# Stick-breaking scores in plain fp32 on the two row halves of TensorE, their first blocks ahead of the former sums, and a reordered last norm

## The reference

```python
def stick_breaking_mixer(h, w_qkv, w_o):
    ...
        z = einsum('bqhd,bshd->bhqs', q_blk, k) * scale
        valid = key_pos[None, :] < q_pos[:, None]
        log_beta = log_sigmoid(z)
        log_keep = where(valid, log_sigmoid(-z), 0.0)
        log_keep_after = cumsum(log_keep, axis=3, reverse=True) - log_keep
        att = where(valid, exp(log_beta + log_keep_after), 0.0)
        return einsum('bhqs,bshd->bqhd', att, v)
    ...

def _rmsnorm(x, g):
    y = x * rsqrt(mean(x * x, axis=-1, keepdims=True) + 1e-6)
    return y * g
```

## Time and profile before

| | |
|---|---|
| time, median of 3 runs | 1160.87 us (1160.63 to 1161.13) |
| profiled execution | 1160.88 us |
| its span | 1159.0 us |
| instructions | 17713 |
| PEld, DVE, ACT, POOL busy | 88%, 70%, 55%, 24% of the span |
| weights and inputs read | 198.43 MB, 172 GB/s over the span |

### The profile page before, as it was taken

One profiled execution on the slowest core, in us unless ns is written; L12 is line 12 of the kernel. 1 busy time (PEld: TensorE's weight loads), 2 busy tenths in 40 slices (PEclk: granted clock), 3 DMA queues, 4 the chain that ended last, 5 costly groups with the idle time before them and its releaser, 6 DMA issues.

```text
span 1159.0 us, 17713 instructions
## 1 busy us (share of the span) xinstructions
PE 1147.4 (99%) x7180; PEld 1020.5 (88%) x7180; DVE 806.4 (70%) x881; ACT 633.2 (55%) x753; POOL 273.2 (24%) x257
## 2 busy tenths in 40 slices
PE   8999999999999999999999999999999999999997
PEld 7999888888998888888899888888889998888885
DVE  6776877776588677767658767777546868777742
ACT  6776565564455456555346656555436765655632
POOL 2000533231123444221111353221110005332100
PEclk9999999999999999999999999999999999999999
DMA  9432655565563255555554355555554326555550
GB/s 341 175 110 74 221 193 199 187 202 190 191 204 110 104 187 182 184 188 198 193 182 146 110 184 191 201 187 182 185 185 176 110 73 220 188 199 193 197 185 37
DMA packets 31515, 201.75 MB, mean 174 GB/s; under 512 B 3680, under 2 KB 5280, under 8 KB 8016
## 3 DMA queue, kind: packets, MB, share of 16 engines
q1 hardware_dynamic: 29088, 196.88, 47.5%
q10 hardware_dynamic: 2032, 3.07, 1.0%
q0 software_dynamic: 320, 0.72, 0.3%
HBM read 198.43 MB, written 1.25 MB: 172 GB/s over the span
## 4 chain that ended last, share of the span: by engine, by line
PE 96%; DVE 2%; DMA 1%; SPq 1%; ACT 0%; issue 0%; POOL 0%; ACTq 0%; DVEq 0%
PE banks L1345 41%; PE banks L1349 21%; PE banks L1333 8%; PE banks L1339 6%; PE banks L1340 6%; PE banks L1341 6%; PE banks L1501 1%; PE banks L1417 1%; PE banks L1515 1%; DMA raw<-w 1%; PE banks L1657 1%; PE banks L1684 1%; PE banks L1669 1%; PE banks L1503 0%; PE banks L1655 0%; SPq L327 0%
## 5 line engine op out<-in xcount | busy, mean ns | idle before, releaser
L869 DVE TENSOR_TENSOR w_lo<-raw,w_hi 128x2048 fp32r<-128x2048 f32 x180 | 442.2, 2461 | 187.9 <-ACT w_hi L509 187.6
L509 ACT ACTIVATE w_hi<-raw 128x2048 fp32r<-128x2048 f32 x183 | 348.5, 1907 | 62.1 <-PE banks L1333 23.4
L1345 PE MATMUL banks<-x_split,w_hi 128*128 128x512 f32 x1408 | 336.8, 391 | 0.0
L1345 PEld LDWEIGHTS banks<-x_split,w_hi 128*128 128x128 f32 x1408 | 258.5, 188 | 50.2 <-DVE w_lo L869 0.4
L1349 PEld LDWEIGHTS banks<-x_split,w_lo 128*128 128x128 f32 x1408 | 181.0, 191 | 7.1
L1349 PE MATMUL banks<-x_split,w_lo 128*128 128x256 f32 x1408 | 184.0, 283 | 0.0
L1345 PE MATMUL banks<-hid_split,w_hi 128*128 128x512 f32 x528 | 129.9, 392 | 0.0
L1345 PEld LDWEIGHTS banks<-hid_split,w_hi 128*128 128x128 f32 x528 | 95.6, 188 | 17.5
L1339 PE MATMUL banks<-x_split,w_hi 128*128 128x256 f32 x384 | 110.0, 286 | 0.0
L1340 PE MATMUL banks<-x_split,w_hi 128*128 128x256 f32 x384 | 108.6, 283 | 0.0
L1341 PE MATMUL banks<-x_split,w_lo 128*128 128x256 f32 x384 | 108.6, 283 | 0.0
(11 more groups left out here) (204 smaller groups left out, 1627.4 us busy)
## 6 DMA issues: line engine op xcount, KB each, us to landing
raw<-w SPq DMA_DIRECT2D x183, 1024.0 KB, 4.9
raw<-w SPq DMA_DIRECT2D x8, 256.0 KB, 5.4
raw<-w SPq DMA_DIRECT2D x2, 512.0 KB, 7.4
k_all<-k_all ACTq DMA_DIRECT2D x1, 960.0 KB, 8.0
x<-x_in SPq DMA_DIRECT2D x4, 128.0 KB, 5.2
x<-x_in SPq DMA_DIRECT2D x2, 256.0 KB, 7.0
rel_bias<-rel_scratch POOLq DMA_DIRECT2D x8, 64.0 KB, 3.1
y_gain<-final_rows ACTq DMA_DIRECT2D x1, 512.0 KB, 6.4
```

What stands on the lines that cost most here:

```text
L509: act.activation(w_hi[u % HI_SLOTS][:, :], raw[slot][:, :], ACT.Copy).then_inc(hi_done, 1)
L869: dve.tensor_tensor(w_lo[slot][:, :], raw[slot][:, :], w_hi[u % HI_SLOTS][:, :].bitcast(FP32), ALU.subtract).then_inc(lo_done, 1)
L1345: return pe.matmul(pair(b), wt[0], xs, start=first, stop=False, skip_group_check=True)
```

## The change

Scores: the splits of keys and queries, their tiles, signals and the zero fill go. Each of the six blocks of 128 x 128 is a plain fp32 matmul of a head's own 64 partitions, `k_all` by `q_all`. The columns are laid out anew, 384 in each of two banks: bank 0 holds the three blocks early keys x early queries of head 0, the same of head 1, and late keys x late queries of head 0; bank 1 holds early keys x late queries of head 0, the same of head 1, and late keys x late queries of head 1. The masks, the sums, ACT's and DVE's operations and the values follow this layout. Two of the six blocks (`logits_begun(p + 1)`, with the masks) now stand ahead of `keep_sums(p)`, and the other four (`logits_rest(p + 1)`) behind it. Last norm: ACT squares all four halves and makes both guesses ahead of any scaling, the mean is one operation with the first half's part done ahead, DVE scales three of the four halves and ACT the fourth, and SyncE stores three.

```diff
...
@@ -239,8 +237,12 @@
-        def head_blocks(v):
-            return v.rearrange("p (h b q) -> p h b q", h=2, b=2)
+        def stick_scores(p):
+            return two_banks[p % 2][:, :].rearrange("p (b s) -> p b s", b=2)[:, :, 0:384]
+        def stick_rows(v):
+            return v.rearrange("p (b s) -> p b s", b=2)
...
@@ -343,9 +345,10 @@
-            for t in range(2):
-                sp.wait_ge(out_ready, t + 1)
-                sp.dma_start(out[:, t, 0:512], y_rows[:, t, 0:512]).then_inc(out_stored, 16)
+            for n, (t, half) in enumerate(((0, 0), (0, 1), (1, 1))):
+                sp.wait_ge(out_ready, n + 1)
+                sp.dma_start(out[:, t, 512 * half:512 * half + 512],
+                             y_rows[:, t, 512 * half:512 * half + 512]).then_inc(out_stored, 16)
@@ -435,19 +438,6 @@
-            def query_zeros(i):
-                if i:
-                    pool.wait_ge(norm.x_new, 16 * i)
-                pool.wait_ge(norm.ss, 2 * i + 1)
-                if i == 0:
-                    pool.wait_ge(cast_done, 2)
-                for h in range(2):
-                    if h:
-                        pool.wait_ge(mixer[i].q_zero, 1)
-                    pool.memset(q_split[others(h), :, h, :].bitcast(FP32), 0.0).then_inc(mixer[i].q_zero, 1)
-                pool.wait_ge(mixer[i].q_zero, 2)
...
@@ -568,13 +556,6 @@
-                def qk_hi(p):
-                    act.wait_ge(m.qk_new, 2 * p + 2)
-                    act.activation(k_split[:, 0, :], k_all[:, p, :], ACT.Copy).then_inc(m.k_hi, 1)
-                    for h in range(2):
-                        act.activation(q_split[own(h), 0, h, :], q_all[own(h), p, :], ACT.Copy).then_inc(m.q_hi, 1)
-                qk_hi(0)
@@ -582,9 +563,9 @@
-                    e, z = buf(0, 768), two_banks[p % 2][:, 0:768]
+                    e = buf(0, 768)
                     act.wait_ge(m.z, p + 1)
-                    t = step(act.activation(e, z, ACT.Abs))
+                    t = step(act.activation(stick_rows(e), stick_scores(p), ACT.Abs))
                     act.wait_ge(act_step, t)
@@ -593,7 +574,7 @@
                     act.wait_ge(m.sums, p + 1)
-                    act.activation(buf(2 + p % 2, 768), two_banks[p % 2][:, 0:768], ACT.Exp).then_inc(m.att, 1)
+                    act.activation(stick_rows(buf(2 + p % 2, 768)), stick_scores(p), ACT.Exp).then_inc(m.att, 1)
...
@@ -767,12 +747,12 @@
-                    act.wait_ge(y_gained, t + 1)
-                    act.wait_ge(y_rstd, t + 1)
-                    act.activation(y_rows[:, t, 512:D], y_part[:, t, :], ACT.Identity,
-                                   scale=small[:, 2, t:t + 1]).then_inc(y_scaled, 1)
-                    act.wait_ge(y_scaled, t + 1)
-                    act.dma_start(out[:, t, 512:D], y_rows[:, t, 512:D]).then_inc(out_stored, 16)
+                act.wait_ge(y_gained, 1)
+                act.wait_ge(y_rstd, 2)
+                act.activation(y_rows[:, 1, 0:512], y_part[:, 1, :], ACT.Identity,
+                               scale=small[:, 2, 1:2]).then_inc(y_scaled, 1)
+                act.wait_ge(y_scaled, 1)
+                act.dma_start(out[:, 1, 0:512], y_rows[:, 1, 0:512]).then_inc(out_stored, 16)
@@ -983,17 +963,7 @@
-                def qk_low(p):
-                    dve.wait_ge(m.k_hi, p + 1)
-                    dve.tensor_tensor(k_split[:, 1, :], k_all[:, p, :], k_split[:, 0, :].bitcast(FP32),
-                                      ALU.subtract).then_inc(m.k_lo, 1)
-                    for h in range(2):
-                        dve.wait_ge(m.q_hi, 2 * p + h + 1)
-                        dve.tensor_tensor(q_split[own(h), 1, h, :], q_all[own(h), p, :],
-                                          q_split[own(h), 0, h, :].bitcast(FP32), ALU.subtract).then_inc(m.q_lo, 1)
...
-                qk_low(0)
@@ -1002,14 +972,12 @@
                     for dst in (sp_hi, buf(1, 768)):
-                        dve.scalar_tensor_tensor(dst, two_banks[p % 2][:, 0:768], 0.0, buf(0, 768),
+                        dve.scalar_tensor_tensor(stick_rows(dst), stick_scores(p), 0.0, stick_rows(buf(0, 768)),
                                                  ALU.max, ALU.add).then_inc(m.softplus, 1)
...
                     dve.tensor_tensor(sp_lo, buf(1, 768), sp_hi.bitcast(FP32), ALU.subtract).then_inc(m.sp_lo, 1)
-                    if p < KT - 1:
-                        qk_low(p + 1)
                     for done in finished(p):
@@ -1225,20 +1193,41 @@
-                for t in range(2):
-                    total, mean = small[:, 0, 4 + t:5 + t], small[:, 0, 6 + t:7 + t]
-                    g, r = small[:, 1, t:t + 1], small[:, 2, t:t + 1]
+                def first_sum(t):
+                    dve.wait_ge(y_squared, 2 * t + 1)
+                    step(dve.tensor_scalar(small[:, 0, 4 + t:5 + t], small[:, 0, 2 * t:2 * t + 1], 1.0 / D, EPS, ALU.mult,
+                                           ALU.add))
+                def row_mean(t):
...
-                    step(dve.tensor_tensor(total, small[:, 0, 2 * t:2 * t + 1], small[:, 0, 2 * t + 1:2 * t + 2], ALU.add))
-                    dve.tensor_scalar(mean, total, 1.0 / D, EPS, ALU.mult, ALU.add).then_inc(y_ms, 1)
-                    dve.tensor_tensor(y_part[:, t, :], y_bank(t, 1)[:, :], y_gain[:, 512:D], ALU.mult).then_inc(y_gained, 1)
+                    dve.scalar_tensor_tensor(small[:, 0, 6 + t:7 + t], small[:, 0, 2 * t + 1:2 * t + 2], 1.0 / D,
+                                             small[:, 0, 4 + t:5 + t], ALU.mult, ALU.add).then_inc(y_ms, 1)
+                def row_rstd(t):
+                    mean, g, r = small[:, 0, 6 + t:7 + t], small[:, 1, t:t + 1], small[:, 2, t:t + 1]
...
+                    dve.wait_ge(y_ms, t + 1)
...
-                    dve.scalar_tensor_tensor(y_rows[:, t, 0:512], y_bank(t, 0)[:, :], r, y_gain[:, 0:512], ALU.mult,
-                                             ALU.mult).then_inc(out_ready, 1)
+                def scaled(t, half):
+                    cols = slice(512 * half, 512 * half + 512)
+                    dve.scalar_tensor_tensor(y_rows[:, t, cols], y_bank(t, half)[:, :], small[:, 2, t:t + 1], y_gain[:, cols],
+                                             ALU.mult, ALU.mult).then_inc(out_ready, 1)
+                first_sum(0)
+                row_mean(0)
+                row_rstd(0)
+                scaled(0, 0)
+                first_sum(1)
+                dve.tensor_tensor(y_part[:, 1, :], y_bank(1, 0)[:, :], y_gain[:, 0:512], ALU.mult).then_inc(y_gained, 1)
+                row_mean(1)
+                scaled(0, 1)
+                row_rstd(1)
+                scaled(1, 1)
...
@@ -1478,43 +1467,48 @@
-                    return bank[2 * (p % 2)], bank[2 * (p % 2) + 1][:, 0:SEQ]
-                def logits(p):
-                    early, late = score_banks(p)
-                    mask = head_blocks(mask_b[:, 0:512])[:, :, 0, :]
-                    pe.matmul(head_blocks(early)[:, :, 0, :], ident_b[:, :], mask, start=True, stop=False,
+                    return bank[2 * (p % 2)][:, 0:384], bank[2 * (p % 2) + 1][:, 0:384]
+                def blocks(p, places):
+                    banks = score_banks(p)
+                    for h, side, at, key, query in places:
+                        last = pe.matmul(banks[side][:, at:at + P], k_all[own(h), p, key:key + P],
+                                         q_all[own(h), p, query:query + P], start=False, stop=True,
+                                         skip_group_check=True)
+                    return last
+                def logits_begun(p):
+                    banks = score_banks(p)
+                    if p < 2:
+                        pe.wait_ge(m.v_new, 2 * p + 2)
+                    else:
+                        pe.wait_ge(m.att, p - 1)
+                    later = mask_b[:, 0:P]
+                    pe.matmul(banks[0].rearrange("p (b q) -> p b q", b=3), ident_b[:, :],
+                              later.unsqueeze(1).to_broadcast([P, 3, P]), start=True, stop=False, skip_group_check=True)
+                    pe.matmul(banks[1][:, 2 * P:3 * P], ident_b[:, :], later, start=True, stop=False,
...
-                    pe.matmul(late, ident_b[:, :], mask, start=True, stop=False, skip_group_check=True)
-                    if p == 0:
-                        pe.wait_ge(m.q_zero, 2)
-                    for key_low, query_low in ((0, 0), (1, 0), (0, 1)):
-                        if query_low:
-                            pe.wait_ge(m.q_lo, 2 * p + 2)
-                        elif key_low:
-                            pe.wait_ge(m.k_lo, p + 1)
-                        else:
-                            pe.wait_ge(m.q_hi, 2 * p + 2)
-                            pe.wait_ge(m.k_hi, p + 1)
-                        kk, qq = k_split[:, key_low, :], q_split[:, query_low, :, :]
-                        pe.matmul(early, kk[:, 0:P], qq.rearrange("p h s -> p (h s)"), start=False, stop=query_low == 1,
```

(48 more changed lines are left out.)

## The result

| | before | after |
|---|---|---|
| time, median (lowest to highest) | 1160.76 us (1160.14 to 1161.63, 7 runs) | 1164.31 us (1163.81 to 1165.37, 7 runs) |
| ratio to before | | 1.0032, 95% interval 1.0022 to 1.0041 |
| profiled execution, its span | 1160.88, 1159.0 us | 1164.84, 1163.0 us |
| instructions of PE | 7180 | 7276 |
| DVE, ACT, POOL busy | 806.4, 633.2, 273.2 us | 785.6, 612.3, 273.2 us |

The change makes the kernel 3.55 us slower, by the medians; forecast were +2.95 us and 1163.8. DVE and ACT lost 21 us of work each and the time went up, since PE is the bound.

What follows compares the result with a forecast made beforehand. PE, busy for 99% of the span, was taken to bound the kernel. Terms 5.9 - 1.2 + 0.3 - 0.7 - 1.35 = +2.95 us gave 1163.8 us; the forecast's own range was 1159.9 to 1167.7, the stated range 1157.0 to 1168.0.

Steps and rivals of the forecast that it cites:

- The mechanism: Whole kernel: PE is busy 99% of the span, so splits taken off DVE and ACT give 0.
- Scores: Each head pair's masks and six fp32 products on PE: 1.64 us against 1.27, +5.9 us for 16 pairs (3.0 to 7.2).
- the visit: PE's change into and out of the half-array form around score products: 0.38 us each, two a pair, bounds 0.29 and 0.42.
- Merged visits: Scores followed directly by weighted values in passes 2, 4, 6: one way out saved, 6 x -0.2 = -1.2 us (-1.8 to 0).
- Pass 7: Last pass of each layer: PE waits for ACT's weights ahead of pair 6's values, +0.3 us for two layers (0 to 0.6).
- Low softplus: Second half of the sums no longer waits for softplus's low half in 8 passes: 8 x -0.09 = -0.7 us (0 at worst).
- New wait for q and k: Ahead of each pair's first score products: PE needs DVE's q and k earlier, 0.7 us to spare, costed at nothing.
- Last norm: Tail behind PE's last matmul: reordered squares, scalings and stores end earlier, -1.35 us (-1.45 to -1.0).
- Cheap visits: Rival: going into and out of the half-array form costs 0.10 us, so the kernel ends faster, 1155.8 us; chance 0.13.
- turning point of 0.29: Price in us of one stay in the half-array form at which the change neither gains nor loses time.
- Halves in turn: Rival: row halves take turns, six score products need 12 slots, +10.3 us on the sum, 1174.1 us; chance 0.08.
- The wait for q and k: Rival: ACT and DVE operations on the new score columns take longer, PE waits in 8 passes, +4, 1167.8 us; chance 0.06.

Runs made afterwards that it cites:

- three-visit kernel: Changed kernel with the four later score blocks split again, two of them between the high and low halves of the former sums: 1170.28 us, ratio 1.0085.
- both groups joined: Changed kernel with masks and all six score blocks behind the former sums, the wait between the two groups kept: 1162.33 us, ratio 1.0016.
- a bank for each head: Changed kernel with each head's three blocks in its own bank, all six behind the sums without a wait, matmul of -1 made per bank: 1159.70 us, ratio 0.9991.
- values apart: Changed kernel with six projection matmuls between score blocks and values of passes 2, 4, 6, twelve output-projection ones in pass 7: 1164.94 us, ratio 1.0034.

## Why the prediction was right

- **The mechanism.** PE bounds the kernel, so the splits taken off DVE and ACT gave nothing: the terms of PE's stream and of the last norm alone make up the whole difference (the sum, below). The three-visit kernel shows the price of visits by itself.
- **Scores, forecast +5.9 us.** Measured 16 x 0.40 = 6.4. The pace of the blocks was right (twos, 0.107 us). The term that was mis-sized is the visit: I took 0.38 us, it is (1.69 - 0.24 - 0.64) / 2 = 0.40 by the pairs and 0.41 by the three-visit kernel. The price of today's scores was a little low as well, 1.27 us for 1.29 in most pairs, which takes some of it back. That the visit came out so near was a choice between the bounds 0.29 and 0.42, with no row that fixed it. The window scores seemed to show a first slot longer by only 0.05 us, 0.16 against 0.107, but their first products have 64 columns and not 128. If half the columns are half the slot, an estimate, the stretch there is the same 0.10 as here; the second 64-column slot, 0.11 us long, is not shortened, so this stays open.
- **Merged visits, forecast -1.2.** 6 x -0.20, shown by the pair of timelines above. The forecast had no row for this; it took one way out as saved, and that is what is saved.
- **Pass 7, forecast +0.3.** ACT's weights come late as worked out. PE's timeline of layer 3, with the idle time before the line:

```profile
948.00 0.72 PE L1476 MATMUL banks<-q_all,k_all 64*128 64x128 f32 x8
949.06 0.66 PE L1406 MATMUL banks<-scratch,v_all 128*64 128x256 f32 x4 [0.35 <-ACT scratch L577]
```

  And from the waits of PE in the kernel after, both layers together:

```profile
PE banks L1406 <- ACT scratch L577: 0.7, 2, 0.3
```

  Values start 1.06 us behind the blocks' start where 0.64 was enough in pass 4, so each layer loses 0.42; against an unmerged visit with its way out (0.20) it is 0.2 more, 0.4 for both. In the three experiments that put more work between the sums and the values of pass 7 (both groups joined, a bank for each head, values apart) it is gone.
- **Low softplus, forecast -0.7.** No second half of the sums is drawn out; -0.7.
- **New wait for q and k, forecast 0.** It isn't among PE's waits. In the tight pass ahead of 74.78 DVE ends `k_all` at 73.75 + 0.41 = 74.16:

```profile
73.75 0.41 DVE L961 TENSOR_TENSOR k_all<-banks,rstd 128x256 f32<-128x256 f32 x1
```

  and PE's blocks of that pass start at 75.10, 0.9 us later; 0.7 was forecast.
- **Last norm, forecast -1.35.** Measured -1.26. The last square starts at 1156.68, as soon as PE's last matmul has ended at 1156.65, and the last scalings follow on it. ACT's share and its store, in the kernel after:

```profile
1156.68 0.60 ACT L744 ACTIVATE scratch<-banks 128x512 f32<-128x512 f32 x1 [0.67 <-PE banks L1322]
...
1158.81 0.72 ACT L752 ACTIVATE y_rows<-y_part,small 128x512 f32<-128x512 f32 x1 [0.74 <-DVE small L1213]
1159.57 0.37 ACTq L755 DMA_DIRECT2D out<-y_rows  x1
```

  and the last store in the kernel before:

```profile
1155.70 0.36 ACTq L775 DMA_DIRECT2D out<-y_rows  x1
```

  From PE's end to that store it is 2.92 us and was 1155.70 - 1151.39 = 4.31, which is 1.39 less, as worked out; from the store to the end of the span it is 3.43 and was 3.30, which takes 0.13 back.

- **The sum.** 6.4 - 1.2 + 0.4 - 0.7 = +4.9 us for the two layers, where the timelines show 2.50 + 2.49 = 5.0. With the norm it is 4.9 - 1.26 = +3.6 us, against 4.0 - 0.27 = 3.7 of the spans and 3.55 of the medians. So the forecast of +2.95 was low by 0.6 us: 0.5 of it is the scores, by the visit, and 0.1 each would be pass 7 and the norm, which is within what the readings can tell.
- **Rivals.** Cheap visits fell by the three-visit kernel (0.41 us, over the turning point of 0.29). Halves in turn fell by the records in twos. The wait for q and k fell by the 0.9 us to spare. What the rival's transposes had shown, a change of form without a gap, stays unexplained: there the work goes on in plain fp32 and never uses two tiles at once, and no run here takes the two apart.

## What to carry to other kernels

Count the times that TensorE goes into and out of a half-array form, not only the columns: here each visit costs 0.40 us, nearly as much as four 128-column fp32 slots, and splitting one short group of products in two to bring a part of it forward turned a draw (a bank for each head) into a loss. Choose the layout of the banks so that a visit needs no wait inside, and put one half form next to another. With PE busy all the time, the work removed from the other engines was worth nothing here, and the place to look for what is left is the tail behind PE's last matmul, where 1.3 us was to be had by itself.

The kernel with a bank for each head and the kernel with the new norm alone both take 1159.7 us, 0.1% less than the kernel before, at the edge of what can be told; the first of them spends 21 us less of DVE and of ACT.

## What the runs showed of the hardware

- A wait of PE for its own last matmuls inside a half-array visit costs 0.33 us (1.63 against 1.30 us for the same six blocks), nearly as much as leaving the form and coming back (0.40). 0.10 of it is the first slot behind the wait, drawn out as at the start of a visit.
- Two products of the two row halves overlap whatever the order in which they are written, within four products: 0.64 to 0.65 us for four in either order.
- In the kernel with a bank for each head, two 128-column fp32r matmuls with a weight load each take 0.17 us (65.06 to 65.23), and the 384-column one behind them 0.06 us more than it would (65.23 to the next start at 65.46, by the 0.39 us of its record against 0.34).
